# A decoder block's FFNs: the gated rows cross between partition bands in SBUF instead of through DRAM

## What is computed

```python
def swiglu(x, wg, wu, wd):
    return (jax.nn.silu(x @ wg) * (x @ wu)) @ wd

h = layer_norm(DN_ALPHA * h + 0.5 * swiglu(h, ffn1_wg, ffn1_wu, ffn1_wd), ln1_g, ln1_b)
mix = token_mixer(h, w_in, ...)          # block-sparse attention and a convolution, gated, one projection
h = layer_norm(DN_ALPHA * h + mix, ln2_g, ln2_b)
h = layer_norm(DN_ALPHA * h + 0.5 * swiglu(h, ffn2_wg, ffn2_wu, ffn2_wd), ln3_g, ln3_b)
```

## Time and profile before

| | |
|---|---|
| median of 3 runs | 2138.96 us |
| the profiled execution | 2138.56 us, its span 2136.8 us |
| PE busy | 2112.4 us, 99% of the span, mean granted clock 0.996 |
| DVE busy | 1828.9 us, 86% |
| ACT busy | 1381.8 us, 65% |
| POOL busy | 184.4 us, 9% |
| `bounce<-h_sq` | 40 DMAs of 256 KB, median 5.4 us to landing |
| `h_in<-bounce` | 160 DMAs of 64 KB, median 2.9 us to landing |
| HBM | 519.45 MB read, 16.78 MB written |

### The profile page before, as it was taken

How to read it: one execution, slowest core, us unless ns; L and a number is a source line. 1 busy time by engine, 2 the same in 40 slices (tenths; PEclk the granted TensorE clock), 3 DMA queues, 4 the chain that set the end, 5 groups by cost and what they waited for, 6 DMA issues and landing times.

```text
span 2136.8 us, 23772 instructions
## 1 busy us (share of the span) xinstructions
PE 2112.4 (99%) x9456; PEld 1749.6 (82%) x9456; DVE 1828.9 (86%) x1380; ACT 1381.8 (65%) x1299; POOL 184.4 (9%) x295
## 2 busy tenths in 40 slices
PE   8999999999999999999999999999999999999998
PEld 6888888888888888888888888888788888888886
DVE  7799999999997798899778874659799999999996
ACT  5677777778775456767554443335577777777773
POOL 0111111110110000000000000000111111101110
PEclk9999999999999999999999999999999999999999
DMA  8688888898886658887556465655688888898892
GB/s 355 231 284 271 273 268 271 281 304 289 276 283 247 263 167 278 270 277 217 187 187 229 175 238 185 242 191 197 217 269 265 275 265 284 295 298 276 292 287 109
DMA packets 87835, 537.75 MB, mean 252 GB/s; under 512 B 12208, under 2 KB 12592, under 8 KB 31920
## 3 DMA queue, kind: packets, MB, share of 16 engines
q1 hardware_dynamic: 68112, 437.69, 54.0%
q0 software_dynamic: 19616, 98.58, 21.7%
HBM read 519.45 MB, written 16.78 MB: 251 GB/s over the span
## 4 chain that ended last, share of the span: by engine, by line
PE 94%; DVE 3%; issue 1%; DMA 1%; ACT 0%; POOL 0%; SPq 0%; DVEq 0%; POOLq 0%; ACTq 0%
PE acc L2101 16%; PE acc L2103 16%; PE acc L2102 16%; PE tb L2101 11%; PE tb L2103 11%; PE tb L2102 11%; PE acc L2041 3%; PE acc L2040 3%; PE acc L2039 3%; PE tb L2087 1%; DVE g_lo L1292 1%; DVE act_sb L1540 0%; DVE res L1547 0%; DMA g_raw<-in_groups 0%; PE tb L2359 0%
## 5 line engine op out<-in xcount | busy, mean ns | idle before, releaser
L1292 DVE TENSOR_TENSOR g_lo<-g_raw,g_hi 128x2048 fp32r<-128x2048 f32 x496 | 1125.5, 2285 | 166.4 <-ACT g_hi L784 165.8
L784 ACT ACTIVATE g_hi<-g_raw 128x2048 fp32r<-128x2048 f32 x496 | 946.6, 1916 | 372.9 <-PE acc L2103 162.8
L2101 PE MATMUL acc<-g_hi,xF_hi 128*128 128x512 f32 x1296 | 510.0, 394 | 8.9 <-DVE g_lo L1615 8.8
L2103 PE MATMUL acc<-g_hi,xF_lo 128*128 128x512 f32 x1296 | 505.6, 390 | 0.0
L2102 PE MATMUL acc<-g_lo,xF_hi 128*128 128x512 f32 x1296 | 505.2, 390 | 0.0
L2101 PEld LDWEIGHTS acc<-g_hi,xF_hi 128*128 128x128 f32 x1296 | 243.9, 188 | 59.3 <-DVE g_lo L1615 9.2
L2103 PEld LDWEIGHTS acc<-g_hi,xF_lo 128*128 128x128 f32 x1296 | 243.7, 188 | 51.4
L2102 PEld LDWEIGHTS acc<-g_lo,xF_hi 128*128 128x128 f32 x1296 | 243.8, 188 | 49.8
L2101 PE MATMUL tb<-g_hi,xF_hi 128*128 128x512 f32 x696 | 273.0, 392 | 3.3 <-ACT c_sb L866 3.3
L2103 PE MATMUL tb<-g_hi,xF_lo 128*128 128x512 f32 x696 | 271.9, 391 | 0.0
L2102 PE MATMUL tb<-g_lo,xF_hi 128*128 128x512 f32 x696 | 271.8, 391 | 0.0
(11 more groups left out here) (155 smaller groups left out, 2217.2 us busy)
## 6 DMA issues: line engine op xcount, KB each, us to landing
g_raw<-in_groups SPq DMA_DIRECT2D x358, 1024.0 KB, 6.9
g_raw<-in_groups POOLq DMA_DIRECT2D x70, 1024.0 KB, 8.2
raw<-in_stream SPq DMA_DIRECT2D x80, 512.0 KB, 4.9
bounce<-h_sq POOLq DMA_DIRECT2D x40, 256.0 KB, 5.4
h_in<-bounce POOLq DMA_DIRECT2D x160, 64.0 KB, 2.9
ln_gb<-in_ln SPq DMA_DIRECT2D x6, 1024.0 KB, 7.8
g_raw<-in_groups SPq DMA_DIRECT2D x4, 512.0 KB, 7.0
res<-in_x_rows SPq DMA_DIRECT2D x1, 2048.0 KB, 15.9
```

The costliest lines, as they stand in the source:

```text
L784: act.activation(g_hi[:, n % RING], source[:], ACT.Copy).then_inc(g_hi_ready, 1)
L1292: dve.tensor_tensor(g_lo[:, n % RING], source[:], f32(g_hi[:, n % RING]), ALU.subtract).then_inc(g_lo_ready, 1)
L2101: pe.matmul(bank, x_hi_ap, g_hi[:, n % RING, blk], start=begin, stop=False, skip_group_check=True)
L2103: return pe.matmul(bank, x_lo_ap, g_hi[:, n % RING, blk], start=False, stop=end, skip_group_check=True)
```

## The change

The tensor `bounce` and the functions `hidden_out` and `hidden_in` go. In their place POOL issues sixteen DMAs per chunk from SBUF to SBUF: for each source band a and each target band c, 32 partitions of `h_sq` to 32 partitions of `h_in`, both t in one DMA, two runs of 512 bytes per partition, 32 KB in all. They are issued behind a single wait for both turned tiles, and all add to one semaphore `hid_in`, in place of `hid_out0`, `hid_out1`, `hid_in0` and `hid_in1`. `hidden_hi` waits for all sixteen for either t. `save` had waited for the write to `bounce` of its t, and now waits for all sixteen too.

```diff
@@ ScalarE: hidden_hi, save @@
-                    act.wait_ge(hid_in[t], 16 * QD * (trips(f, b) + 1))
+                    act.wait_ge(hid_in, 16 * QD * QD * (trips(f, b) + 1))
                     act.activation(by_step(hT_hi, b, t), h_in[:, t], ACT.Copy).then_inc(h_hi, 1)
...
-                act.wait_ge(hid_out[t], 16 * trips(f, b))
+                act.wait_ge(hid_in, 16 * QD * QD * trips(f, b))
                 fork(f, b, c_sb[:, t], bank_sets[b % 2][:, BX], behind)
@@ GpSimd @@
-            def hidden_out(f, b):
-
-                for t in range(TT):
-                    pool.wait_ge(squared, TT * trips(f, b) + t + 1)
-                    pool.dma_start(bounce[t].rearrange("a p c b n -> (a p) (c b n)"),
-                                 h_sq[:, t].rearrange("p c b n -> p (c b n)")).then_inc(hid_out[t], 16)
-
-            def hidden_in(f, b):
-
-                for t in range(TT):
-                    pool.wait_ge(hid_out[t], 16 * (trips(f, b) + 1))
+            def hidden_across(f, b):
+
+                pool.wait_ge(squared, TT * (trips(f, b) + 1))
+                for a in range(QD):
                     for c in range(QD):
-                        pool.dma_start(h_in[STEP * c:STEP * (c + 1), t].rearrange("p a b n -> p a (b n)"),
-                                     bounce[t, :, :, c].rearrange("a p b n -> p a (b n)")).then_inc(hid_in[t], 16)
+                        pool.dma_start(h_in[STEP * c:STEP * (c + 1), :, a].rearrange("p t b n -> p t (b n)"),
+                                       h_sq[STEP * a:STEP * (a + 1), :, c].rearrange("p t b n -> p t (b n)")).then_inc(
+                                           hid_in, 16)
...
-                    hidden_out(f, b)
-                    hidden_in(f, b)
+                    hidden_across(f, b)
```

More of the change, by code:

```diff
@@ L288, in build @@
     assert SPLIT0 == 2 * (N1 % RING)
-    bounce = nc.dram_tensor("bounce", (TT, QD, STEP, QD, BLK, STEP), F32, kind="Internal").ap()
     kept = nc.dram_tensor("kept", (P, TT, D), F32, kind="Internal").ap()
@@ L444, in build @@
         filled = sem("filled")
-        hid_out = [sem(f"hid_out{t}") for t in range(TT)]
-        hid_in = [sem(f"hid_in{t}") for t in range(TT)]
+        hid_in = sem("hid_in")
         res_loaded = sem("res_loaded")
```

## The result

The changed kernel takes 2149.32 us (median of 6 runs, 2147.16 to 2149.88) against 2138.67 us of the kernel before on the same chip (6 runs, 2138.36 to 2141.66). The ratio is 1.0047, with a 95% interval of 1.0036 to 1.0057: 10.7 us slower. The profiled execution took 2149.29 us, with a span of 2147.5 us; that of before 2138.56 and 2136.8, so the two profiles are 10.7 us apart as well.

The account below looks back on a forecast made before the run. TensorE was taken to bound the kernel, with 94% of the chain. First FFN +5.9 and second FFN +1.8 gave +7.7 us on 2138.56, so 2146.3 (2146.6 for the median), range 2139 to 2152.

Parts of the forecast that it names:

- The ring: POOL's descriptor memory takes twelve of the new DMAs; the thirteenth is held until the first twelve are all in.
- The moved wait: In chunk 1, save waits for all sixteen DMAs, so TensorE waits at P7, some 8 us sooner than before.
- First FFN, +5.9: Chunk 1, first FFN: rows in at 79.5, TensorE waits 3.3 us at P7, slow clock 2.6: +5.9 us.
- The bound of 6.5 us for the twelfth: Chunk 1, first FFN, upper bound: the twelfth DMA takes the fifth old read's 6.5 us to land: +8.5 us.
- Second FFN, +1.8: Chunk 1, second FFN: rows in at 1521.8, wait 5.1 and clock 2.6 us, 7.7 in place of 5.9: +1.8 us.
- Full chunks, 0: Other 18 chunks: rows in 8 us early, accumulating load with 3.4 us to spare, so no new wait: 0 us.
- Less traffic through DRAM, 0: Whole kernel: less DRAM traffic gains 0 us, as no other wait of TensorE is on a DMA.
- the small version (+2.3): Chunk 1: same mechanism, first FFN waits 1.3 us at full clock, second adds 1.0; 2141.3 us, chance 0.2.
- The one with room given back one by one: POOL's descriptor memory frees room singly or holds all sixteen, so the last four leave earlier; 2145 or 2142.5 us, chance 0.1.
- The faster one: Chunk 1: SBUF-to-SBUF DMAs land in 2.5 us even under load; -4.6 us, 2134.4 us, chance 0.12.
- the third rival: Chunk 1: small DMAs land in 2.5 us despite SP's loads, making the kernel faster: 2134.4 us, chance 0.12.
- The rival in which the twelfth is caught in both places: Chunk 1, both FFNs: the twelfth DMA lands late behind SP's loads; +8.5 and +5 us, 2152.5 us, chance 0.1.

Follow-up runs that it names:

- two experiments: Changed kernel with four semaphores, one per source band, instead of one: 2139.95 us; changed kernel with 2048 instead of 1024 bytes of descriptor memory: 2139.29 us.
- the second profile: The changed kernel run and profiled once more with nothing changed: 2150.34 us.
- the best through DRAM: Kernel before, trip through DRAM kept, with 2048 instead of 1024 bytes per partition for POOL's descriptors: 2134.67 us, ratio 0.9981 to the kernel before.
- The version with both links out: Changed kernel with `h_sq` in 4 KB of its own (no wait of save) and four semaphores instead of one: 2133.94 us, ratio 0.9979 to the kernel before.
- its second profile: The kernel before run and profiled once more with nothing changed: 2136.94 us.

## Why the prediction was right

The forecast, 2146.3 us (2146.6 for the median of the runs) with 2139 to 2152, has 2149.3 inside, and the mechanism was the one that happened. By its steps:

- **The ring.** Right in every part. Twelve DMAs leave, the thirteenth leaves about 0.4 us after all twelve are in, and is held in each of the 20 chunks, the count of twelve came true, and the reason given, room that comes back by semaphore, stands by two experiments.
- **The moved wait.** Right: `c_sb` waits for the DMA, and TensorE at P7 in both FFNs. Before's wait at the second half of g1 is gone.
- **First FFN, +5.9.** It was +7.8. Counted from the second turned tile (61.83 in the forecast, 64.71 measured), the twelfth was issued 6.8 us after it (forecast 6.6), but took 5.2 us to land where 3.3 had been taken from the old fourth read. This is the mis-sized term: 1.9 us. The last four then took 7.9 us from the thirteenth's issue to the last landing, against 7.5. Wait 5.77 instead of 3.3, clock 2.0 instead of 2.6. The bound of 6.5 us for the twelfth held.
- **Second FFN, +1.8.** It was -0.2. The last landing was 16.2 us behind the turned tile, where the forecast had 17.1 (1521.8 - 1504.70), since the twelve were in 7.6 us after the first issue, not 8.4. Wait 4.07 instead of 5.1, clock 1.9 instead of 2.6.
- **Full chunks, 0.** Right in the profiled execution, but not in every one: the second profile has two short waits there, told above. They are for plain loads, not for the rows or the accumulating load whose margins the forecast worked out. In the full chunk of the earlier trace rows the sixteenth leaves at 192.9 and lands in 1.7 us, and the rows are used at 203.87, some 9 us later; and the accumulating load leaves at 193.41, is in 7.9 us later and is used at 204.91: 3.6 us to spare, forecast 3.4.

```profile
193.41 1.00 POOL L1962 DMA_DIRECT2D g_raw<-in_groups  x1
```

```profile
203.87 1.13 ACT L800 ACTIVATE hT_hi<-h_in 128x512 fp32r<-128x512 f32 x2
204.91 1.90 ACT L782 ACTIVATE g_hi<-g_raw 128x2048 fp32r<-128x2048 f32 x1
```

- **Less traffic through DRAM, 0.** Right within what these runs tell: 0.7 us between the best version on the chip and the best through DRAM.

The two errors of the places, +1.9 and -2.0, cancel in the profiled pair. The sum of 7.6 against 7.7 is therefore partly luck. The medians differ by 10.7, 3 us more than the forecast, and the floors show why. The version with both links out takes 2133.94 us. With 7.8 and 6.0 on top (56.21 - 48.38 and 52.03 - 46.02), the changed kernel comes to 2147.8, 1.5 us less than its median. The waits in full chunks can be a part of this rest: outside the trips the second profile is 1.6 us longer than the version with both links out (1395.43 and 581.75 against 1394.54 and 581.06), the first 0.2. The remainder is open. The kernel before comes to 2133.94 + 2.6 = 2136.5 if its wait goes like that of its second profile, and to 2140.2 like that of the first: its median, 2138.7, lies between. I had taken the dear one of the two, 5.9 us, for what the place always costs, because the only profile of before showed it. This is the second thing mis-sized, and it hides in the "+1.8": against the mean cost of the place before (4.4 us), the second FFN is not -0.2 but +1.6.

Of the rivals, the small version (+2.3) fell by the first FFN, where it had a wait of 1.3 us at full clock. In the second FFN it had the landing better than the forecast: 1521.8 in the forecast is 17.1 us behind the turned tile and 1521.0 in the rival 16.3, and it was 16.2. The one with room given back one by one fell by the break behind the twelfth in all chunks. The faster one, landing in 2.5 us even under load, fell by landings of 5.2 to 6.3 us. The twelfth DMA of the first FFN's chunk 1 by itself, first in the changed kernel, then in the one whose loads are held (issue to landing; one DMA, so its three numbers are equal):

```profile
DMA to landing us min/median/max: 5.2/5.2/5.2
```

```profile
DMA to landing us min/median/max: 1.8/1.8/1.8
```

The Trainium skill ("DMA: Bandwidth & Descriptors", Queues, rings and completion order) lets each DMA engine take turns between its queues packet by packet, a packet being typically 9 to 17 descriptors. The prediction took this to mean that the small DMAs would hardly be delayed, which the runs refute (1.8 us against 5.2), and gave it the third rival's chance. What the page states is not refuted. The thirteenth DMA was issued at 77.09, yet from 78.0 to 80.5 the DMA engines moved packets of SP's queue (the profile's hardware queue) alone, 148 or about nine for each of 16 engines; POOL's come in from 80.5 on, beside SP's:

```profile
q1 hardware_dynamic: 148, 1.08, 103.5%
```

If one such record is a descriptor, which no run here shows, that is one turn of the page's size. A turn behind loads of 1 MB was then simply longer than the prediction thought.

The rival in which the twelfth is caught in both places came half true. In the first FFN it was caught (5.2 of the 6.5 us), in the second it was not (0.8 us sooner than forecast, all twelve together).

## What to carry to other kernels

When a copy is made in one step instead of two, look at what the first step released: here the early release of a buffer was worth more than the trip that was saved, and 4 KB per partition of its own made it needless. Before rewriting a burst of DMAs, look for a break in its issue for which nothing is named; here it was want of descriptor room, and one number gave 4 us in the kernel before. And profile the kernel before twice where a sum rests on one wait: 2.3 or 3.3 us of wait was 2.6 or 6.2 us of time.

## What the runs showed of the hardware

- With 1024 bytes of descriptor memory POOL holds seven DMAs of 64 KB or twelve of 32 KB, and the next waits until every DMA of the oldest semaphore is in. The thirteenth waited 1.65 to 5.26 us in the changed kernel and the version with `h_sq` of its own. With four semaphores for sixteen DMAs it is not held in chunk 1, and shorter holds (to 1.8 us) are left in full chunks; with 2048 bytes there are two of under 0.2 us.
- Holding SP's weight loads back in chunk 1 until the rows were in cost TensorE nothing there (its trips are 48.40 and 46.05 us, the floors), and gave 14.9 us. The loads had time to spare, the rows had none. Its one `g_lo` wait, 1.9 us, is at 267.56, some 190 us after the held loads were let go.
- The clock behind waits of not much different length went two ways. After 2.3 us (before, second profile) 20 matmuls in 4.55 us ran at 1.00; after 3.3 (first profile) the clock stood at 0.50. A wait of 2.80 us in the version with four semaphores was followed by the two windows below: 0.57 for 3 us, then mostly full. In these rows one us more of wait brought up to 2.6 us more of slow clock, so the price of a wait is even less certain than the wait itself.

```profile
1523.00:1526.00 3.00, 2.75 (x7) 0.57 1.04 434
1526.00:1530.00 4.00, 4.00 (x18) 0.90 0.40 98
```

- The start of the kernel varies between executions: by 1.9 us between the two profiles of before, 0.4 between the two of the changed kernel, and 3 us over all eleven. A difference of two single profiles holds that much chance.
